# Split weights: the products with a weight's high part come first, those with its low part last, and each kind has a wait of its own

## What is computed

```python
x = x + 0.5 * swiglu(rms_norm(x, ffn1_norm), w_gate, w_up, w_down)      # hidden width 2816
h = rms_norm(x, mix_norm)
fq, fk, fv, f_logit, sq, sk, sv, g_fox, g_sb = split_columns(h @ w_in)
y_fox = forgetting_attention(rms_norm(fq, q_norm), rms_norm(fk, k_norm), fv, log_sigmoid(f_logit + bias))
y_sb = stick_breaking_attention(sq, sk, sv)
x = x + (sigmoid(g_fox) * (y_fox @ w_branch_fox) + sigmoid(g_sb) * (y_sb @ w_branch_sb)) @ w_out
x = x + 0.5 * swiglu(rms_norm(x, ffn2_norm), ...)
x = x + sigmoid(rms_norm(x, ple_norm) @ w_ple_gate) * (p @ w_ple_proj)
# second block: norm, w_in, short and long convolutions (by spectra), latent attention, gated merge, w_out
```

## Time and profile before

| | |
|---|---|
| median of 3 runs | 1690.03 us (1689.97 to 1690.15) |
| profiled execution | 1690.89 us |
| its span, first to last instruction | 1688.8 us |
| TensorE busy | 1677.1 us (99%), 7690 matmuls |
| VectorE, ScalarE, GpSimd busy | 1025.6, 639.0, 716.0 us |
| granted TensorE clock | 1.000 on average |

### The profile page before, as it was taken

How to read it: one execution, slowest core, us unless ns; L and a number is a source line. 1 busy time by engine, 2 the same in 40 slices (tenths; PEclk the granted TensorE clock), 3 DMA queues, 4 the chain that set the end, 5 groups by cost and what they waited for, 6 DMA issues and landing times.

```text
span 1688.8 us, 21189 instructions
## 1 busy us (share of the span) xinstructions
PE 1677.1 (99%) x7690; PEld 1370.8 (81%) x7690; DVE 1025.6 (61%) x1217; ACT 639.0 (38%) x895; POOL 716.0 (42%) x303
## 2 busy tenths in 40 slices
PE   9999999999999999999999999999999999999999
PEld 7887888887788888888888888888777668888887
DVE  6767566527665446457675566785564753969441
ACT  5222222225565756322322222213446754343221
POOL 3444344434334431444444344443455433444443
PEclk9999999999999999999999999999999999999999
DMA  5332233325221320243423323332252023233243
GB/s 195 102 109 91 78 100 100 104 84 195 87 63 51 101 75 26 91 134 100 140 90 109 102 88 100 101 102 94 90 187 75 26 95 127 90 100 99 90 143 118
DMA packets 43103, 171.04 MB, mean 101 GB/s; under 512 B 4969, under 2 KB 5353, under 8 KB 41740
## 3 DMA queue, kind: packets, MB, share of 16 engines
q1 hardware_dynamic: 39024, 148.13, 27.3%
q10 hardware_dynamic: 3996, 21.73, 3.7%
HBM read 159.22 MB, written 10.62 MB: 101 GB/s over the span
## 4 chain that ended last, share of the span: by engine, by line
PE 68%; issue 22%; POOL 6%; DVE 2%; ACT 1%; DMA 0%; POOLq 0%; DVEq 0%; SPq 0%; ACTq 0%
PE psum L307 20%; PE psum L309 20%; PE psum L308 20%; POOL wlo L273 6%; PE psum L1201 1%; PE psum L1768 1%; PE psum L1745 1%; PE psum L1219 1%; PE psum L752 1%; PE psum L737 0%; PE psum L1191 0%; PE psum L723 0%; DVE psum L445 0%; PE psum L1717 0%; DMA xT<-x_dram 0%
## 5 line engine op out<-in xcount | busy, mean ns | idle before, releaser
L273 POOL TENSOR_TENSOR wlo<-raw,whi 128x1024 fp32r<-128x1024 f32 (+2 forms) x258 | 663.7, 2573 | 886.5 <-ACT whi L295 885.9
L295 ACT ACTIVATE whi<-raw 128x1024 fp32r<-128x1024 f32 (+2 forms) x259 | 286.1, 1105 | 703.8 <-PE psum L309 693.6
L307 PE MATMUL psum<-h_hi,whi 128*128 128x512 f32 x1360 | 537.3, 395 | 3.4 <-POOL wlo L273 2.5
L309 PE MATMUL psum<-h_hi,wlo 128*128 128x512 f32 x1360 | 529.7, 389 | 0.0
L308 PE MATMUL psum<-h_lo,whi 128*128 128x512 f32 x1360 | 529.6, 389 | 0.0
L307 PEld LDWEIGHTS psum<-h_hi,whi 128*128 128x128 f32 x1360 | 255.4, 188 | 64.2 <-POOL wlo L273 4.9
L308 PEld LDWEIGHTS psum<-h_lo,whi 128*128 128x128 f32 x1360 | 255.4, 188 | 53.9 <-issue 2.4
L309 PEld LDWEIGHTS psum<-h_hi,wlo 128*128 128x128 f32 x1360 | 255.3, 188 | 53.5
L307 PE MATMUL psum<-mid_hi,whi 128*128 128x512 f32 x352 | 137.2, 390 | 0.0
L309 PE MATMUL psum<-mid_hi,wlo 128*128 128x512 f32 x352 | 137.0, 389 | 0.0
L308 PE MATMUL psum<-mid_lo,whi 128*128 128x512 f32 x352 | 136.9, 389 | 0.0
(11 more groups left out here) (388 smaller groups left out, 2376.2 us busy)
## 6 DMA issues: line engine op xcount, KB each, us to landing
raw<-wk_dram SPq DMA_DIRECT2D x220, 512.0 KB, 3.5
raw<-wd_dram SPq DMA_DIRECT2D x32, 704.0 KB, 4.1
raw<-wp_dram SPq DMA_DIRECT2D x8, 640.0 KB, 3.8
x_scratch<-xT ACTq DMA_DIRECT2D x2, 2048.0 KB, 9.0
spectra_scratch<-spec_out ACTq DMA_DIRECT2D x4, 1024.0 KB, 6.7
xT<-x_scratch ACTq DMA_DIRECT2D x8, 512.0 KB, 4.5
spec<-spectra_scratch ACTq DMA_DIRECT2D x2, 2048.0 KB, 10.1
xT<-x_dram SPq DMA_DIRECT2D x4, 512.0 KB, 7.5
```

Of the source, the lines that this page charges most:

```text
L273: pool.tensor_tensor(wlo[s][:, 0:w], raw[s][:, 0:w], whi[s][:, 0:w].bitcast(F32), ALU.subtract).then_inc(lo_ready, 1)
L295: act.activation(whi[s][:, 0:w], raw[s][:, 0:w], ACT.Copy).then_inc(hi_ready, 1)
L307: pe.matmul(dst, s_hi, m_hi, start=start and i == 0, stop=False, **kw)
L309: last = pe.matmul(dst, s_lo, m_hi, start=False, stop=stop and i == n - 1, **kw)
```

## The change

All edits are in TensorE's instruction stream. (1) A new `high_part_first` puts the products of a unit with `whi` first (two for each chunk), then a wait for `lo_ready`, then the products with `wlo`. The wait before a unit is for `hi_ready` only. `linear`, `linear_piece` and, in its own code, `linear_by_token` use it; a piece of a unit has the same order within the piece. With `chunk_ready` the order stays chunk by chunk and the wait for the low part stands within the first. (2) `tensor_first_tiles` starts with the pieces of `h_hi` alone and takes up `first_lo`, `h_lo`, `whi` and `wlo` of unit 1 as they come; one matmul on zeros fewer. (3) The norm's sum in the feed-forward part moves from before a unit to behind the first two chunks of it. Line numbers of the new kernel are larger; 315, 316 and 320 take the place of 307, 308 and 309.

```diff
+        def high_part_first(pe, dst, u, chunks, m_hi, m_lo, start=True, stop=True, await_low=True):
+            chunks = list(chunks)
+            for c, a, b in chunks:
+                pe.matmul(dst, a, m_hi[:, c, :], start=start and c == chunks[0][0], stop=False)
+                pe.matmul(dst, a, m_lo[:, c, :], start=False, stop=False)
+            if await_low:
+                pe.wait_ge(lo_ready, u + 1)
+            for c, a, b in chunks:
+                last = pe.matmul(dst, b, m_hi[:, c, :], start=False, stop=stop and c == chunks[-1][0])
+            return last
...
         def linear(pe, dst, u, m_hi, m_lo, n, first=0, chunk_ready=None, ready_base=0, signal=True):
 
-            for c, (a, b) in enumerate(weight_chunks(u, first, n)):
-                if chunk_ready is not None:
+            chunks = ((c, a, b) for c, (a, b) in enumerate(weight_chunks(u, first, n)))
+            if chunk_ready is None:
+                last = high_part_first(pe, dst, u, chunks, m_hi, m_lo)
+            else:
+                for c, a, b in chunks:
                     pe.wait_ge(chunk_ready, ready_base + c + 1)
-                last = products(pe, dst, [(a, b, m_hi[:, c, :], m_lo[:, c, :])], start=c == 0, stop=c == n - 1)
+                    last = high_part_first(pe, dst, u, [(c, a, b)], m_hi, m_lo, start=c == 0, stop=c == n - 1,
+                                           await_low=c == 0)
...
             for t, b in enumerate(banks, first):
                 if b in bank_ready:
                     pe.wait_ge(*bank_ready[b])
-                terms = [(s_hi[:, 2 * j + c, t * P:(t + 1) * P], s_lo[:, 2 * j + c, t * P:(t + 1) * P],
-                          whi[s][:, c * 512:(c + 1) * 512], wlo[s][:, c * 512:(c + 1) * 512]) for c in range(2)]
-                last = products(pe, bank(b), terms, start=j == 0, stop=j == of - 1)
+                for c in range(2):
+                    tokens, w = slice(t * P, (t + 1) * P), whi[s][:, c * 512:(c + 1) * 512]
+                    pe.matmul(bank(b), s_hi[:, 2 * j + c, tokens], w, start=j == 0 and c == 0, stop=False)
+                    pe.matmul(bank(b), s_lo[:, 2 * j + c, tokens], w, start=False, stop=False)
+            pe.wait_ge(lo_ready, u + 1)
+            for t, b in enumerate(banks, first):
+                for c in range(2):
+                    last = pe.matmul(bank(b), s_hi[:, 2 * j + c, t * P:(t + 1) * P], wlo[s][:, c * 512:(c + 1) * 512],
+                                     start=False, stop=j == of - 1 and c == 1)
...
             def tensor_idle(self, pe):
                 pe.wait_ge(x_updated, 1)
-                for _ in range(9):
+                for _ in range(8):
...
-                        pe.wait_ge(lo_ready, up + 2 * f + 1)
+                        pe.wait_ge(hi_ready, up + 2 * f + 1)
...
-                        if half == 0 and f == 1:
-                            self.norm.tensor(pe)
-                        pe.wait_ge(lo_ready, up + 2 * f + 2)
+                        pe.wait_ge(hi_ready, up + 2 * f + 2)
                         if half or f > 2:
                             pe.wait_ge(self.mid, freed)
-                        linear(pe, bank(1 + apart), up + 2 * f + 1, h_hi, h_lo, DT)
+                        if half == 0 and f == 1:
+                            linear_piece(pe, bank(1 + apart), up + 2 * f + 1, h_hi, h_lo, 0, 2, DT)
+                            self.norm.tensor(pe)
+                            linear_piece(pe, bank(1 + apart), up + 2 * f + 1, h_hi, h_lo, 2, DT - 2, DT)
+                        else:
+                            linear(pe, bank(1 + apart), up + 2 * f + 1, h_hi, h_lo, DT)
```

More of the change, by code:

```diff
@@ L310, in products @@
             return last
+        def high_part_first(pe, dst, u, chunks, m_hi, m_lo, start=True, stop=True, await_low=True):
[8 more added lines that the diff above has]
+            return last
         def linear_piece(pe, dst, u, m_hi, m_lo, first, n, of):
-            for c, (a, b) in enumerate(weight_chunks(u, first, n), first):
-                last = products(pe, dst, [(a, b, m_hi[:, c, :], m_lo[:, c, :])], start=c == 0, stop=c == of - 1)
+            chunks = ((c, a, b) for c, (a, b) in enumerate(weight_chunks(u, first, n), first))
+            last = high_part_first(pe, dst, u, chunks, m_hi, m_lo, start=first == 0, stop=first + n == of)
             if first + n == of:
@@ L512, in tensor_first_tiles @@
                 self.tensor_idle(pe)
[L513 to L527, removed]
-                                        start=c == 0, stop=c == DT - 1)
-                        if c == DT - 1:
+                hi, lo = (first_hi, whi[1]), (first_lo, wlo[1])
@@ new lines, in on_high, with on_low @@
+                def on_high(g, k, weight):
+                    pe.matmul(bank(2 + g), weight[g][:, k * P:(k + 1) * P], h_hi[:, k, :],
+                              start=k == 0 and weight is hi, stop=False)
+                def on_low(g, k):
+                    return pe.matmul(bank(2 + g), hi[g][:, k * P:(k + 1) * P], h_lo[:, k, :], start=False, stop=k == DT - 1)
+                for k in range(2):
+                    pe.wait_ge(gained_hi, k + 1)
+                    on_high(0, k, hi)
+                pe.wait_ge(lo_ready, 1)
@@ new lines, in tensor_first_tiles @@
+                for k in range(2):
+                    on_high(0, k, lo)
+                    pe.wait_ge(gained, k + 1)
+                    on_low(0, k)
+                pe.wait_ge(hi_ready, 2)
+                for k in range(2):
+                    on_high(1, k, hi)
+                    on_low(1, k)
+                pe.wait_ge(gained_hi, 3)
+                on_high(0, 2, hi)
+                on_high(0, 2, lo)
+                pe.wait_ge(lo_ready, 2)
+                for k in range(2):
+                    on_high(1, k, lo)
@@ L530, in tensor_first_tiles @@
+                for k in range(2, DT):
+                    pe.wait_ge(gained_hi, k + 1)
+                    for g in range(1 if k == 2 else 0, 2):
+                        on_high(g, k, hi)
+                        on_high(g, k, lo)
+                    pe.wait_ge(gained, k + 1)
+                    for g in range(2):
+                        last = on_low(g, k)
+                        if k == DT - 1:
                             last.then_inc(unit_done, 1)
@@ L561, in down_tile @@
                     def down_tile(b, k, first=False):
-                        pe.wait_ge(lo_ready, down + b + 1 + k)
+                        pe.wait_ge(hi_ready, down + b + 1 + k)
                         pe.wait_ge(x_updated, self.x_base + 8 * half + b - 1 + k)
@@ L937, in tensor @@
                 for j in range(4):
-                    pe.wait_ge(lo_ready, BASE["fox_v"] + j + 1)
+                    pe.wait_ge(hi_ready, BASE["fox_v"] + j + 1)
                     if j == 0:
@@ L1110, in tensor @@
                     pe.wait_ge(fox.out_hi, 2 * HEADS)
-                    pe.wait_ge(lo_ready, BASE["sb_v"] + j + 1)
+                    pe.wait_ge(hi_ready, BASE["sb_v"] + j + 1)
                     linear_by_token(pe, (4, 5, 6, 7), BASE["sb_v"] + j, j, 4, h_hi, h_lo,
@@ L1386, in tensor_first_out @@
                     pe.matmul(bank(0), hi, merged_hi[:, c, :], start=c == 0, stop=False)
+                    if c == 0:
+                        pe.wait_ge(lo_ready, self.out_base + 1)
                     pe.matmul(bank(0), lo, merged_hi[:, c, :], start=False, stop=False)
@@ L1478, in tensor_part @@
                 if g == 0:
-                    pe.wait_ge(lo_ready, u + 1)
+                    pe.wait_ge(hi_ready, u + 1)
                 if b >= 2:
@@ L2839, in tensor_last_out @@
             def tensor_last_out(self, pe):
+                pe.wait_ge(lo_ready, self.out_base + DT)
                 for g in range(2):
```

26 lines of the change are left out of this document (13 added, 13 removed).

## The result

| | before | changed |
|---|---|---|
| median | 1690.1 us (10 runs) | 1694.26 us (10 runs) |
| profiled execution, its span | 1690.89, 1688.8 us | 1694.56, 1692.5 us |
| ratio | | 1.0025, interval 1.0017 to 1.0033 |

The account below looks back on a forecast made before the run. TensorE, busy 99% of the span, was taken to bound nearly everything. Terms 1.2 + 1.46 + 1.31 + 0.4 - 0.45 = 3.9 us took 1690.89 to 1687.0, and 0.86 less for the median gave 1686.1; range 1684.9 to 1689.2.

Parts of the forecast that it names:

- The start: First two units: the 15th product comes at 11.13 instead of 12.36, a gain of 1.2 us (0.9 to 1.3).
- The norm's sum: Feed-forward part: the sum moves behind six products, 1.36 us; the start's gain brings it back within 0.2, so 0.
- `fox_f`: Wait for the low part before this unit goes: 1.38 us plus 0.08 for the restart, 1.46 gained.
- the second unit of `fox_k`: Wait for the low part before this unit goes: 1.23 us plus 0.08 for the restart, 1.31 gained.
- The step that failed: At fox_v's bank 5, ScalarE's chain behind the sums was said to move with TensorE as a whole.
- The rival "gain is taken back": Up to fox_v, a later wait takes back the 2.8 us of fox: median 1688.9, or 1687.5 with half lost; chance 0.27.
- `fox_v`'s banks: Banks 4 and 5: eight products instead of six behind bank 5's wait, so the unit ends later, a loss of 0.45 us.
- The stick-breaking attention: After 616.18 TensorE's wait for a low part goes: 0.34 us, with the restart 0.42; counted as 0.4 gained.
- the second block: First unit: the wait before 1220.05 goes, but TensorE stands again at 1224.68; gain 0, at most 0.6 us.
- My 0.08 for a restart: Wherever TensorE really stops at a wait, restarting costs 0.08 us more, by the distance at 8.39.
- The added waits: TensorE's stream: 308 more waits, taken as 0 us, with an upper bound of 3.1 us.
- the rival that ended on the slower side: Waits in the middle of units cost TensorE time; at 0.04 us each, 1698.4. Chance 0.08, of which 0.05 slower by over 0.2%.

Follow-up runs that it names:

- run 11: Kernel before with the new start alone (eight passes on zeros, first two units in the new order): 1690.34 us, ratio 1.0001.
- run 12: Kernel before with the new start, and the feed-forward norm's sum behind the first two chunks of its unit, old order: 1689.11 us, ratio 0.9993.
- run 1: Changed kernel with the forgetting attention's projections (fox_q, fox_f, fox_k, fox_v) in the old order behind one low-part wait: 1688.23 us, ratio 0.9988.
- run 4: Kernel before with a second, long-passed wait for the low part in the middle of every linear unit and piece (293 waits): 1690.25 us, ratio 1.0000.
- run 6: Changed kernel, but TensorE waits for the low part again before fox_f, and only there: 1695.53 us, ratio 1.0030.
- run 8: Kernel before with seven GpSimd subtractions each made to wait for VectorE's pair of copies: 1691.23 us, ratio 1.0007.
- run 2: Changed kernel with seven GpSimd subtractions, from the third unit of fox, each made to wait for VectorE's pair of copies: 1686.52 us, ratio 0.9978.
- run 7: Changed kernel with the four products of bank 4 in fox_v's first unit done five times over, filling the wait for bank 5: 1692.51 us.
- run 10: Changed kernel with one GpSimd wait for the first copies before fox_k's second subtraction, and bank 4's low-part products ahead of bank 5's wait: 1686.09 us.
- run 9: Changed kernel with a single GpSimd wait, before its subtraction for fox_k's second unit, until VectorE's first pair of copies is done: 1686.51 us, ratio 0.9978.

## Why the prediction was wrong

- **The start** was right: 1.20 us in the trace (1.2 forecast), the 15th product at 11.17 (11.13). **The norm's sum** was called 0, and in the changed kernel it is; run 11 shows that the start's 1.2 rests on it. I had counted both moves and not said that the one without the other is worth nothing.
- **`fox_f`** gained 2.71 - 1.20 = 1.51 between the two profiles (forecast 1.46), **the second unit of `fox_k`** 1.13 (1.31). As mechanisms both were right, and both low parts were in time. But the size at `fox_f` is that of one execution. Wherever TensorE waits for the low part at this place, it is idle for 1.23 us in the profile of before and 1.22 in that of run 12, executions of 1690.89 and 1689.98 that are 0.6 to 0.9 above their medians, and for 0.22 to 0.56 in runs 1, 4, 6, 8 and 11. Before and run 4, which is the kernel before with passed waits added:

```profile
396.92 0.69 DVE L2368 TENSOR_TENSOR spec_out<-spec_real,spec_out 128x512 f32<-128x512 f32 x1
```

```profile
396.95 2.89 POOL L273 TENSOR_TENSOR wlo<-raw,whi 128x1024 fp32r<-128x1024 f32 x1 [4.79 <-ACT whi L295]
```

```profile
396.84 2.39 POOL L273 TENSOR_TENSOR wlo<-raw,whi 128x1024 fp32r<-128x1024 f32 x1 [4.37 <-ACT whi L295]
```

```profile
399.29 0.50 PE L307 MATMUL psum<-h_hi,whi 128*128 128x512 f32 x1 [0.26 <-POOL wlo L273]
```

In the profile of before, GpSimd meets a row that VectorE began 0.03 us earlier and takes 2.89, not 2.39. Between 395 and 405 run 4 is 0.97 us faster, so in a median execution `fox_f` is worth about 1.51 - 0.97 = 0.54, an estimate. The forecast then took 0.86 off once more for the median: much the same microsecond twice.
- **The step that failed** is what was said of the time behind them: that ScalarE's chain "moves with TensorE as a whole". In the changed kernel it moved with TensorE by 2.71 and not by the 1.13 of the second unit, and the place that was to cost 0.45 cost 8.3. In run 2, without the meetings, the wait for bank 5 ends 450.74 - 446.88 = 3.86 us sooner than before, so the chain does move with TensorE once the copies are free. I had followed `whi` up to that unit and asked only whether it would be late for TensorE. I had not asked what would be early: behind that unit ScalarE no longer waited for TensorE ahead of its next `whi`, GpSimd's subtraction came 0.9 us sooner relative to VectorE's copies, and the margin was 0.33. The rows for that were in the trace of before, in a pair of 5.03 us as well, the first, under two subtractions.
- **The rival "gain is taken back"** named the place, the bank waits of `fox_v`, but had its price bounded by the 2.8 us gained there. A wait can take back no more than the lead only if the other engines are where they were. Here they were 5.63 us later (run 2), and 2.2 came on top by the clock (run 7). From run 2's median that makes 1686.52 + 5.63 + 2.22 = 1694.37, against 1694.26 measured.
- **`fox_v`'s banks** cost 0.45 in the forecast and 0.42 in run 10; in the changed kernel the far longer wait hides it.
- **The stick-breaking attention** gained 4.24 - 3.85 = 0.39 (0.4). Another 0.22 came ahead of it (4.46 to 4.24), at a wait for the low part that I had left out as too short to count. In **the second block** the 0.45 gained before 1220.05 is given back by 1224.68, as forecast (0), and 3.88 - 3.66 = 0.22 comes later, in two steps of 0.1 near 1237 and 1268. The 0.22 at 572, in the kernel before (a row not shown ahead, and the product 13 steps behind it):

```profile
572.05 0.39 PE L309 MATMUL psum<-h_hi,wlo 128*128 128x512 f32 x1
572.32 0.50 PE L307 MATMUL psum<-h_hi,whi 128*128 128x512 f32 x1
...
575.22 0.39 PE L307 MATMUL psum<-h_hi,whi 128*128 128x512 f32 x1
```

From 572.05 to 575.22 are 3.17 us for 13 steps, in place of 2.95. The row at 572.32 is 0.04 late and has no idle time in brackets, and yet the stop costs 0.22, spread over the products behind it. My 0.08 for a restart counted only the first of these.
- **The added waits** at 0 were right (run 4), so the rival that ended on the slower side had the sign by a mechanism that isn't there.

So the list of places was right for a kernel in which VectorE and GpSimd don't meet. Run 2 is that kernel and gains 3.8 us (3.9 forecast); run 10, with the bank mended, gains 4.2 (the terms without the bank's 0.45 are 4.37). That the totals fit so well is partly luck. In a median execution `fox_f` gives 0.9 less than the term says. Four things that weren't forecast make up for it: the two 0.22; a start that in run 4's profile of the old order is about 0.3 later than in that of before; and 0.3 us outside the span, since the executions of runs 2, 8, 9 and 10, those with a wait on GpSimd, are 1.8 us longer than their spans and the others 2.1. Why they are is open.

## What to carry to other kernels

When a change lets the busiest engine run ahead, list which engine waited for it, because these waits also kept other pairs of engines apart; look at what each freed engine issues next and whether that meets an instruction it can't run beside. A margin of 0.33 us between two such instructions is a bound of the prediction like any other, and a loss behind it isn't limited by the gain: it can renew itself in later rounds and bring the clock down. The cheap remedy is a wait on the engine that has slack: with the low part wanted late, one wait on GpSimd was worth 7.7 us. And before a wait's length from one profile goes into a forecast for the median, see whether that execution is a typical one: the 0.6 to 0.9 us by which the profile of before exceeded its median lay in a wait that the change removes.

## What the runs showed of the hardware

- Beside a subtraction of 2.40 us on GpSimd a copy of 0.42 us on VectorE took up to 2.55, and two subtractions in a row stretched a pair to 5.03. GpSimd's own rows stayed at 2.36 to 2.40 there. In the profile of before, where VectorE's row began 0.03 us earlier than the subtraction, GpSimd's took 2.89.
- TensorE idle for 3.77 us, with 1.26 and 0.53 idle shortly before, fell to the level of 1.2 GHz: granted clock 0.50 from 452 to 456, its products 0.42 us apart until 457.35, 2.22 us lost. The same place with the 3.77 filled kept 1.00, though the other two waits stood.
- A stop of TensorE by 0.04 us cost 0.22 over the 13 steps from 572.05 on: the next step takes 0.34 in place of 0.2267, and the 11 behind it 0.233 on average.
- 293 passed waits added to TensorE's stream had no measurable cost (0 within 1.5 us).
